# The first norm applied at eviction, the gated cells' preparation in pieces inside the first product, and narrower waits in the second block

## The reference, cut to what matters

```
h = rmsnorm(x, norm1_w);  z = h @ w_in
fq, fk, fv, ff, mq, mk, mv, mi, mf, mo = split(z)
att  = forgetting_attention(fq, fk, fv, ff + bias)
mqk  = silu(causal_depthwise_conv(concat(mq, mk)))      # 4 taps
cell = sigmoid(mo) * mlstm_chunkwise(mq_c, mk_c, mv, mi + .., mf + ..)
x = x + concat(norm(att), norm(cell)) @ w_out
x = x + peer_ffn(rmsnorm(x, norm2_w), ...)
# second block
u = rmsnorm(x); p = u @ w_in_2
o_dn = deltanet(p[:dn])   # conv, silu, l2norm of q and k heads, chunked delta rule
o_rw = rwkv7(p[dn:])      # decays, grams of r, k, kk, a inside chunks, state scan
x = x + concat(o_dn, o_rw) @ w_out_2
x = x + memory_cross_attention(rmsnorm(x), rmsnorm(mem), wq, wk, wv, wo)
x = x + relu(rmsnorm(x) @ w1)**2 @ w2;  out = rmsnorm(x)
```

## Time and profile before

| | us |
|---|---|
| median of 3 runs | 3748.93 |
| lowest, highest | 3744.07, 3749.57 |
| profiled execution | 3747.8 |
| its span, first to last instruction | 3746.1 |
| TensorE busy | 3559.0 |
| VectorE, ScalarE, GpSimd busy | 2332.6, 1473.8, 75.0 |

### The profile page before, as it was taken

One profiled execution on the slowest core, in us unless ns is written; L12 is line 12 of the kernel. 1 busy time (PEld: TensorE's weight loads), 2 busy tenths in 40 slices (PEclk: granted clock), 3 DMA queues, 4 the chain that ended last, 5 costly groups with the idle time before them and its releaser, 6 DMA issues. The chain is left out here.

```text
span 3746.1 us, 51944 instructions
## 1 busy us (share of the span) xinstructions
PE 3559.0 (95%) x21282; PEld 3108.5 (83%) x21282; DVE 2332.6 (62%) x2658; ACT 1473.8 (39%) x1288; POOL 75.0 (2%) x110
## 2 busy tenths in 40 slices
PE   8997799999999999999999999987989989999998
PEld 7986589999988888888888799975656878888887
DVE  4544546987757776666666765466674556666666
ACT  3333333345543333433333434443332433333333
POOL 1000000000000000000000000000100000000000
PEclk9998899999999999999999999988999999999999
DMA  4551344556667676555555455421114435555554
GB/s 184 177 193 68 112 159 175 203 181 230 223 249 245 235 259 206 202 202 202 200 206 199 153 180 181 158 102 45 46 57 146 146 135 191 190 189 187 187 189 145
DMA packets 122754, 649.44 MB, mean 173 GB/s; under 512 B 10721, under 2 KB 43873, under 8 KB 49537
## 3 DMA queue, kind: packets, MB, share of 16 engines
q1 hardware_dynamic: 116370, 621.26, 47.3%
q0 software_dynamic: 6256, 26.34, 1.9%
HBM read 619.77 MB, written 27.79 MB: 173 GB/s over the span
## 5 line engine op out<-in xcount | busy, mean ns | idle before, releaser
L2294 DVE TENSOR_TENSOR w_low<-ring,w_high 128x2048 fp32r<-128x2048 f32 (+1 forms) x540 | 1233.0, 2284 | 911.8 <-ACT w_high L1220 911.2
L1220 ACT CAST w_high<-ring 128x2048 fp32r<-128x2048 f32 (+1 forms) x540 | 1026.1, 1901 | 1700.4 <-PE pairs L2547 1240.8
L2545 PE MATMUL pairs<-x_t,w_high 128*128 128x256 f32 x2608 | 746.3, 286 | 14.5 <-DVE w_low L2294 11.5
L2546 PE MATMUL pairs<-x_t,w_high 128*128 128x256 f32 x2608 | 740.7, 284 | 0.0
L2547 PE MATMUL pairs<-x_t,w_low 128*128 128x256 f32 x2608 | 740.5, 284 | 0.0
L2590 PE MATMUL quad<-x_t,w_high 128*128 128x512 f32 x1984 | 703.5, 399 | 9.9 <-DVE w_low L2294 9.9
L2545 PE MATMUL pairs<-w_high,act_high 128*128 128x512 f32 x1568 | 612.0, 390 | 5.4 <-ACT arena L769 3.5
L2546 PE MATMUL pairs<-w_low,act_high 128*128 128x512 f32 x1568 | 611.4, 390 | 0.0
L2547 PE MATMUL pairs<-w_high,act_low 128*128 128x512 f32 x1568 | 611.0, 390 | 0.0
L2591 PE MATMUL quad<-x_t,w_low 128*128 128x256 f32 x1984 | 557.7, 281 | 0.0
L2545 PEld LDWEIGHTS pairs<-x_t,w_high 128*128 128x128 f32 x2608 | 501.9, 192 | 17.9 <-DVE w_low L2294 11.8
(11 more groups left out here) (535 smaller groups left out, 2935.5 us busy)
## 6 DMA issues: line engine op xcount, KB each, us to landing
ring<-pu SPq DMA_DIRECT2D x128, 1024.0 KB, 4.8
ring<-pv SPq DMA_DIRECT2D x128, 1024.0 KB, 4.8
ring<-f SPq DMA_DIRECT2D x128, 1024.0 KB, 4.8
ring<-win SPq DMA_DIRECT2D x48, 1024.0 KB, 4.8
ring<-dn SPq DMA_DIRECT2D x32, 1024.0 KB, 4.8
ring<-rw SPq DMA_DIRECT2D x24, 1024.0 KB, 4.8
ring<-wout SPq DMA_DIRECT2D x16, 1024.0 KB, 4.8
ring<-wq SPq DMA_DIRECT2D x16, 1024.0 KB, 4.8
```

Of the source, the lines that this page charges most:

```text
L1220: nc.scalar.copy(WH[s % 2][:, 0:w], flat(ring[s])[:, 0:w]).then_inc(ev["split_high"], 1)
L2294: v.tensor_tensor(WL[s % 2][:, 0:w], flat(ring[s])[:, 0:w], WH[s % 2][:, 0:w].bitcast(F32), ALU.subtract).then_inc(ev["split_low"], 1)
L2545: mm(out, stat[0], mov[0], start=start, stop=False, skip_group_check=True)
L2546: mm(out, stat[0], mov[1], start=False, stop=False, skip_group_check=True)
```

## The change

It has these parts:
- The weight of the first norm is not loaded as a row or spread; x itself is turned, and the weight is applied as a column at eviction: four instructions of 128x128 a bank on ScalarE and on VectorE in place of one of 128x512 each.
- The convolution is cut in eleven pieces of three operations, each behind a low half in units 2 to 5. SiLU runs on ScalarE in unit 5, the spreading of the decays, the exponentials, the query-key products and the turning of keys and shares in units 6 to 9. The sigmoid stands behind the attention heads, and the load of the second norm's weight waits longer on GpSimd's queue.
- The head norms are summed with a column selector of 16 columns as weight and 256 tokens moving, 16 products that add up in one bank, then turned back. Some small VectorE steps move from unit 5 of `rw` to units 2 and 4.
- In RWKV-7, two new signals (`grams_ready` after 10 of the last 14 multiplies, `bks_ready` after 12) replace the one at the end; the addition stands between, and the turning stands behind the first pair of grams and uses side banks.
- `xk`, `xv` and `xq` wait for the eviction before the newest; the last addition is in two halves; rows of the memory are turned in two sets of four banks, not three.

```
+            def mix_act(j, s):
+                if (j, s) == (5, 2):
+                    act.wait_ge(*nth("conv_out", 1))
+                    nc.scalar.activation(flat(MQC[:, 0:4]), flat(MQC[:, 0:4]), ACT.Silu)
...
+            def weighed_rows(banks):
+                for n in banks:
+                    act.wait_ge(ev["turned"], n + 1)
+                    for m in range(4):
+                        kt = 4 * (n // 2) + m
+                        ins = nc.scalar.mul(XTH[:, kt, ...], PQ[:, n % 4, m * P:(m + 1) * P], col1("norm1", kt))
+                    ins.then_inc(ev["rows_high"], 1)
...
+            def mix_dve(j, s):
+                step = 4 * j + s - 10
+                if 0 <= step < 11:
+                    conv(3 * step, min(3 * step + 3, 32))
...
-            turn_into(0, "x_weighted", 2, SCN, "win", True)
+            turn_into(0, "diag", 1, X, "win", True)
...
-            product("win", 6, 6, False)
+            product("win", 6, 1, False, following=decays_spread)
+            product("win", 7, 1, False)
+            product("win", 8, 1, False, following=keys_queries)
+            product("win", 9, 1, False, following=shares_turned)
+            product("win", 10, 2, False)
...
-                        for t in range(NT):
-                            n = 16 * t + 4 * g + i
-                            ins = mm(PQ[:, 0, n:n + 1], SQD[g % 3][:, i, t * P:(t + 1) * P], ONES[:, 0:1], ...)
+                    n = 4 * g + i
+                    ins = mm(PQ[0:16, 0, 0:T], COL16[:, 15 - n:31 - n], SQD[g % 3][:, i, :], start=(n == 0), stop=(n == 15), ...)
...
-                if first == 0 and name not in ("rw",):
+                if first == 0 and name not in ("rw", "xk", "xv", "xq"):
                     pe.wait_ge(ev["dve_free"], DVE0[name])
...
-            pool.wait_ge(*nth("conv_out", 1))
+            pool.wait_ge(*nth("mix_ready", 2))
```

More of the change, by code:

```diff
@@ L1997, in final_add @@
             def final_add(i):
+                cols = slice(BLK * FINAL[i], BLK * (FINAL[i] + 1))
+                if i == 3:
+                    dve.wait_ge(ev["last_half"], 1)
+                    o.tell(v.tensor_tensor(X[:, 1, cols], X[:, 1, cols], o_bank(15)[:, 1], ALU.add), ev["last_added"])
                 dve.wait_ge(ev["o2_used"], 13 + i)
-                cols = slice(BLK * FINAL[i], BLK * (FINAL[i] + 1))
-                for t in range(NT):
+                for t in range(NT if i < 3 else 1):
                     ins = v.tensor_tensor(X[:, t, cols], X[:, t, cols], o_bank(12 + i)[:, t], ALU.add)
@@ L2387, in gates, with conv @@
                 o.done(v.tensor_tensor(LF, TM[:, 2:4, :], TM[:, 0:2, :], ALU.subtract), ev["log_f"])
+            def conv(first, last):
+                for i in range(first, last):
+                    tap, n = i // 8, i % 8
+                    if i == 0:
+                        dve.wait_ge(ev["act_free"], 4)
+                        dve.wait_ge(ev["dve_free"], 4)
+                    elif i == first:
+                        dve.wait_ge(o.order, o.n[id(o.order)])
+                    if tap == 0:
+                        ins = v.tensor_scalar(MQC[:, n, :], MQK[:, n, 0:T], col1("cw", 4 * n), col1("cb", n), ALU.mult, ALU.add)
+                    else:
+                        ins = v.scalar_tensor_tensor(MQC[:, n, :], MQK[:, n, tap:tap + T], col1("cw", 4 * n + tap),
+                                                     MQC[:, n, :], ALU.mult, ALU.add)
+                    o.tell(ins, o.order)
+                if last == 32:
+                    dve.wait_ge(o.order, o.n[id(o.order)])
+                    o.tell(v.nop(), ev["conv_out"])
@@ L2389, in _ @@
             for j in range(12):
                 if j < 11:
-                    lows("win", j + 1, (0, 1))
+                    for s in range(2):
+                        lows("win", j + 1, (s,))
+                        mix_dve(j, s)
                 ps = half("win", j)
@@ L2409, in _ @@
                 elif j < 11:
-                    lows("win", j + 1, (2, 3))
+                    for s in range(2, 4):
+                        lows("win", j + 1, (s,))
+                        mix_dve(j, s)
                 if j == 1:
@@ L3156, in _ @@
             pe.wait_ge(ev["identity"], 1)
-            pe.wait_ge(ev["norm1_in"], 16)
-            for n in range(4):
-                ins = mm(PP[:, n // 2, n % 2, :], ONES[0:1, :], NROW[:, BLK * n:BLK * (n + 1)], start=True, stop=True)
-            ins.then_inc(ev["norm1_spread"], 1)
-            turn_into(0, "x_weighted", 2, SCN, "win", True)
+            turn_into(0, "diag", 1, X, "win", True)
             pe.wait_ge(ev["rows_low"], 8)
```

329 lines of the change are left out of this document (175 added, 154 removed).

## The result

| us | before | changed |
|---|---|---|
| median of the runs made with the prediction | 3749.25 (4 runs) | 3684.88 (4 runs) |
| lowest to highest | 3744.07 to 3749.60 | 3684.46 to 3689.78 |
| span of the profiled execution | 3746.1 | 3682.7 |
| mean granted clock of TensorE | 0.975 | 0.984 |

The ratio is 0.9834, with a 95% interval of 0.9817 to 0.9852. The forecast was 3695.9 within 3686 to 3710. The sign and the places were right, the size was short by 11: 53 forecast, 64 measured. Over all 13 timings of it the median is 3686.1 (3683.7 to 3689.8), and that is the number the experiments are set against. The kernel before was timed beside every experiment too; its 36 timings have a median of 3748.1, so the saving over all timings is 62.0.

What follows compares the result with a forecast made beforehand. TensorE, busy 95% of the span, was taken as the bound, with time to gain only where it waits, runs slow or does droppable work. Savings less one cost sum to 53.0 off 3747.8; median 3695.9 us, range 3686 to 3710.

Steps and rivals of the forecast that it cites:

- A: At the start, turning x itself and applying the norm weight at eviction saves 5.0 us (0 to 6.5).
- Rival 1: At the start, GpSimd's masks keep VectorE out until 20.0; 2 us lost instead of 5 saved, 3703 us; chance 0.15.
- B: In the first product, cutting the convolution into pieces behind low halves saves 9.5 us (8 to 9.5).
- rival 4: In chunks with moved pieces, VectorE exceeds its room of 5.0 us; slower than before, 3756 us; chance 0.03.
- C: Gated-cell matrix work moved into the first product costs 4.9 us, between 4.4 and 8.8.
- D: At the first attention head, exponentials start earlier and some lower clock may go; saves 6.5 us (4.5 to 7.5).
- E: Behind the last attention head, the gated cells' preparation moves into the product; saves 17.3 us (16 to 18.7).
- F: Head norms by 16 products of 256 columns with 16 selector columns; saves 2.7 us (2 to 3.5).
- G: Six small VectorE steps before the first gram move behind an earlier unit's diagonals; saves 3.4 us (0 to 3.4).
- H: In both RWKV-7 halves, gram pairs start earlier, 3.7 us saved each; 7.4 us together (5 to 10).
- I: Three memory-attention products no longer wait for the newest eviction, and the last addition is split; saves 6.1 us (4 to 6.2).
- rival 2: Splits buy no time in the serial parts and the clock does not come back; 12 us less saved, 3708; chance 0.13.

Runs made afterwards that it cites:

- the two controls: The changed kernel run again with no edit, on two further occasions; measured 3687.39 us and 3685.46 us.
- shares_late: Changed kernel with the gated cells' query-key products, shares, turnings and copies moved back behind the last attention head; measured 3691.39 us.
- grams_late: Changed kernel with the RWKV grams in their old order: addition first, all 14 multiplies, turning, copies, then the pairs; measured 3699.14 us.
- conv_sizes: Changed kernel with the convolution in pieces of 4, 12 and 16 operations instead of eleven of three; measured 3687.82 us, one run.

## Why the prediction was right, and where it fell short

- **A, 5.0:** 5.1 by the third chunk in the first execution, but 3.5 and 3.7 in the two controls, 4.1 in the mean. All ten kernels of the experiments have their third chunk between 37.95 and 38.47, so the first execution is the exception. The step that failed is that it left out the lower clock at the product's start. The diagonals were not held up at all: 0.48 for both, while GpSimd worked. Rival 1 is out. The first chunk starts at 20.97, 1.3 later than I had it, since the evictions began at 13.93 and pushed the weight cast back; it did not matter, as the third chunk binds.
- **B, 9.5:** 9.3, undone. The room of 5.0 a chunk, on which rival 4 rested, was measured and is right.
- **C, 4.9 paid:** 4.9, from the stretch behind the third chunk. The 28 instructions that shares_late removed cost 3.3; the spread and what comes with it the rest. Rival 3 is out: TensorE's waits inside the product are gone.
- **D, 6.5:** 5.5. The exponential comes 4.5 earlier as worked out (0.03 behind its maxima); the clock gave back 1.0, where I had taken 2.0 of at most 3, as the lower clock only moved to 315.
- **E, 17.3:** 18.7, 18.7 and 17.2. Right in sum, and too evenly spread in my mind: half of the moved chain is worth next to nothing net.
- **F, 2.7:** four groups of 1.91 and 0.61 are 8.25. Before, 48 took 8.31 and the last 16 took 1.84, not the 2.8 that I had scaled from the others: 10.15. So 1.9. The step that failed is scaling the price of the last sixteen from a group that had gaps in it.
- **G, 3.4:** 3.4, shown with its two parts.
- **H, 7.4:** 13.4 by undoing it, 14.6 between the traces. This is the term that was mis-sized. The step is "the second pair of grams starts at about 2615.2, saved 3.7 each": it moved the instructions with the durations that the earlier trace rows show. These durations (2.08 and 1.94) were those of the lower clock, a consequence of the very wait that the change removes. In place of 3.7 a half the undone order costs 6.7, 3.5 of it clock. I had allowed for the clock in D and E and not here, where a later row of the same stage (a group of 1.14 at 2623.79) would have told.
- **I, 6.1:** the waits were right at 6.2, and the term gave 6.9 between the traces. The same omission, but small: the clock that does not fall. The other 1.7 of the table's 8.6 are a stretch at the lower clock ahead of the memory products, behind a wait that the change left at 2.74.
- **The sum:** 53.0 forecast. H fell short by 7.2, E by 0.9 and I by 0.8; A was 0.9 too much, B 0.2, D 1.0 and F 0.8. That gives 59.0. The table's sum is 61.3, and the rest is where the lower clock falls in stages that nobody touched, the 1.7 above among them. That the total came as near as it did is in part luck: a miss of 7.2 in one term was met by 2.9 too much in four others. The forecast's own range of 3687 to 3704 misses the result of 3684.88, and the full one of 3686 to 3710 has it 1.1 under its lower end, well inside the interval of the ratio; the 3686.1 of all 13 timings lies just in it. The low end was too high above all because of H: its upper end, 10, lies under the 13.4 and 14.6 measured.
- **The other rivals:** rival 2 was wrong the other way round: its one true point, that the clock decides in the serial parts, speaks for a larger gain, in H above all. Rival 4 would have needed 7.3 of side work a chunk; the room was 5.0, and TensorE has no wait between the third chunk and the scores.

## What to carry to other kernels

Where a change takes away a wait of TensorE, do not move the instructions behind it with their old durations. Look whether they ran at the lower clock, and price them by the same instruction at the higher clock elsewhere in the stage; the end of a long wait can pay twice. How much more it pays varied here from 1.1 to 3.6 a wait, so give it a range. And where a serial chain is moved into a product, price each link of it on its own: a link that is short in the chain and as long inside the product can stay where it is.

## What the runs showed of the hardware

- **The length of a wait does not give the price of the lower clock behind it.** Beyond the wait itself, a gram stage lost 3.5 with a wait of 6.70 (old order), 1.1 and 1.6 with 8.01 and 9.14 (new order), and 3.2 to 3.6 with 4.06 (new order, seven stages). The price goes with how long the clock stays low: 0.50 over nine us behind a wait of 4.06, 0.80 behind one of 8.01.
- **Nor does it alone decide whether the lower clock comes.** Before the first pair of grams TensorE waited 2.93 in 15 stages, and its groups then took 1.13 to 1.14; in 7 it waited 4.06, and they took 2.08. But a wait of 2.74, some 22 us behind the second gram stage, is in all 14 traces, and the granted clock over the 4 us behind it was 0.50, 0.57 and 0.68 in three of them (grams_late, before, conv_sizes) and 1.00 in eleven.
- **A stretch at the lower clock can shorten the next wait.** In the 15 stages with 2.93 the granted clock over the 14 us that end 8 before the first pair was 0.88, in the 7 with 4.06 it was 1.00. So kernels that differ only far ahead differ here by 4.4 to 4.7 a stage. Where only the second stage was long, 3.0 of it came back in the stages on either side; where both were, 3.0 and 4.5 of 9. The shorter wait and the stretch ahead always go together, so no run here shows which of them keeps the clock up behind the wait. Why the clock is low over part of 2673 to 2680, where TensorE is busy for all of the 7.00, is open; in all three executions of the changed kernel the stage was 1.6 longer there.
- **Contention goes both ways.** GpSimd's `tensor_tensor` at 18.59 took 2.51 beside VectorE's low half (18.54 to 20.83), where it takes 0.41 in the earlier trace rows; VectorE's small step was held by 2.2 until a clearing ended. The small diagonals met GpSimd's masks without any delay.
